# A hybrid attention, state space and expert layer on one core: first products, one gate product, expert choice and one more held weight tile moved

## The reference

```python
h = h + hybrid_mixer(rms_norm(h, norm1_g), ...)   # conv, state space, attention, gates
tok = rms_norm(h, norm2_g)
top_v, top_i = lax.top_k(tok @ w_router + b_router, 4)
top_w = softmax(top_v)
for e in range(32):
    gu = tok @ w_gate_up[e] + b_gate_up[e]         # 1024 x 2048
    gate, up = minimum(gu[:, :1024], 7), clip(gu[:, 1024:], -7, 7)
    act = (up + 1) * (gate * sigmoid(1.702 * gate))
    out += dense_w[:, e:e+1] * (act @ w_down[e] + b_down[e])   # 1024 x 1024
h = rms_norm(h + out, final_g)
```

## Time and profile before

| | us |
|---|---|
| median of 3 timed runs | 1452.72 |
| the runs | 1448.02, 1452.72, 1452.91 |
| the profiled execution | 1448.05 |
| its span, first to last instruction | 1446.2 |
| TensorE busy in the span | 1385.3 |
| VectorE busy | 361.2 |
| ScalarE busy | 233.5 |

### The profile page before, as it was taken

How to read it: one execution, slowest core, us unless ns; L and a number is a source line. 1 busy time by engine, 2 the same in 40 slices (tenths; PEclk the granted TensorE clock), 3 DMA queues, 4 the chain that set the end, 5 groups by cost and what they waited for, 6 DMA issues and landing times.

```text
span 1446.2 us, 14861 instructions
## 1 busy us (share of the span) xinstructions
PE 1385.3 (96%) x6176; PEld 600.4 (42%) x6176; DVE 361.2 (25%) x807; ACT 233.5 (16%) x495; POOL 50.4 (3%) x33
## 2 busy tenths in 40 slices
PE   7999999989999999999999999999999999999997
PEld 6887754444444443333333333333333333333332
DVE  5665855124300122111111111111112112111211
ACT  2116532124300121000100010001001001000101
POOL 1502220000000000000000000000000000000000
PEclk9999999999999999999999999999999999999999
DMA  9455321253156369999999999999999999999995
GB/s 361 178 189 190 117 103 44 115 234 117 68 208 270 146 252 427 426 432 433 433 428 431 433 433 427 430 434 431 430 430 429 431 427 431 429 429 432 432 425 221
DMA packets 25824, 475.01 MB, mean 328 GB/s; under 512 B 4176, under 2 KB 5360, under 8 KB 6800
## 3 DMA queue, kind: packets, MB, share of 16 engines
q1 hardware_dynamic: 25728, 474.28, 78.3%
q10 hardware_dynamic: 48, 0.03, 0.0%
HBM read 473.22 MB, written 1.08 MB: 328 GB/s over the span
## 4 chain that ended last, share of the span: by engine, by line
PE 69%; DMA 29%; DVE 1%; ACT 1%; issue 0%; SPq 0%; DVEq 0%
DMA weights<-in_w_gate_up_dram 28%; PE ps L990 23%; PE ps L673 7%; PE ps L1014 6%; PE ps L553 6%; PE ps L756 4%; PE ps L764 4%; PE ps L578 4%; PE ps L527 2%; PE ps L869 2%; PE ps L847 2%; PE ps L1024 2%; PE ps L950 2%; PE ps L604 1%; PE ps L615 1%; DMA weights<-in_w_blocks_dram 1%
## 5 line engine op out<-in xcount | busy, mean ns | idle before, releaser
L990 PE MATMUL ps<-weights,hnT 128*64 128x512 f32 x2000 | 450.9, 606 | 32.0 <-DMA weights<-in_w_gate_up_dram 32.0
L990 PEld LDWEIGHTS ps<-weights,hnT 128*64 128x64 f32 x2000 | 144.8, 139 | 322.4 <-issue 264.7
L1014 PE MATMUL ps<-weights,hnT 128*64 128x512 f32 x1016 | 225.1, 595 | 1.0 <-ACT hnT L1093 1.0
L1093 ACT ACTIVATE hnT<-ps 128x512 f32<-128x512 f32 (+1 forms) x95 | 49.9, 526 | 785.1 <-PE ps L527 562.0
L1703 DVE TENSOR_SCALAR ssmT<-ps 128x512 f32<-128x512 f32 x32 | 22.1, 692 | 473.6 <-PE ps L990 473.6
L1014 PEld LDWEIGHTS ps<-weights,hnT 128*64 128x64 f32 x1016 | 70.1, 137 | 133.3 <-issue 126.8
L673 PE MATMUL ps<-weights,hnT 128*128 128x512 f32 x224 | 98.0, 594 | 0.0
L553 PE MATMUL ps<-hnT,weights 128*128 128x272 f32 x352 | 81.4, 393 | 0.0
L553 PEld LDWEIGHTS ps<-hnT,weights 128*128 128x128 f32 x352 | 66.7, 190 | 14.0 <-issue 0.4
L1093 ACT ACTIVATE arena<-ps 128x512 f32<-128x512 f32 (+5 forms) x89 | 40.7, 494 | 161.4 <-PE ps L673 81.1
L1024 PE MATMUL ps<-hnT 64*128 64x512 f32 x256 | 63.6, 615 | 0.8 <-DVE hnT L1730 0.8
(11 more groups left out here) (224 smaller groups left out, 920.8 us busy)
## 6 DMA issues: line engine op xcount, KB each, us to landing
weights<-in_w_gate_up_dram SPq DMA_DIRECT2D x53, 4096.0 KB, 20.4
weights<-in_w_down_dram SPq DMA_DIRECT2D x28, 4096.0 KB, 17.4
weights<-in_w_blocks_dram SPq DMA_DIRECT2D x28, 2048.0 KB, 7.9
weights<-in_w_gate_up_dram SPq DMA_DIRECT2D x6, 3072.0 KB, 16.8
weights<-in_w_gate_up_dram SPq DMA_DIRECT2D x8, 2048.0 KB, 8.7
weights<-in_w_down_dram SPq DMA_DIRECT2D x4, 2048.0 KB, 15.4
arena<-in_w_gate_up_dram SPq DMA_DIRECT2D x5, 1024.0 KB, 13.5
weights<-in_w_gate_up_dram SPq DMA_DIRECT2D x4, 1024.0 KB, 7.0
```

The costliest lines, as they stand in the source:

```text
L990: mm = pe.matmul(bank(4 + b)[64 * a:64 * a + 64, :], xe[:, 2 * (k % 4) + k // 4, :], w[:, FF * b + 512 * a:FF * b + 512 * a + 512], start= ...
L1014: mm = pe.matmul(bank(7)[64 * c:64 * c + 64, :], actT[:, P * j + SLOTS * a:P * j + SLOTS * a + SLOTS], pair[kk % 2][:, 512 * c:512 * c + 5 ...
L1093: return nc.scalar.activation(o, i, ACT.Copy)
```

## The change

Five things are changed:

- The first block is laid out in four quarters for tiles 0 to 3, and its first half is requested as two quarters with a semaphore each. TensorE runs 16 products of a matrix of ones ahead of tile 0.
- `filler(1)` stands between `scores(0)` and `scores(1)`, and each pair's filler is the next in number. ScalarE's and VectorE's parts that belong to fillers move one pair forward with them.
- In the expert choice the positions are made ahead of `dense_w`, the constant is added in the table `slots`, and the counts take two products. `start_bias(0)` no longer waits for the tokens. The total count and the turn of `dense_w` stand behind the gather.
- One more chunk is held, for expert 25.
- To make room, some buffers of the expert stage share memory (`act` with `upc`, `actT` with `sig`, `xrow` with `y_sb`), and `bdn` and `gf_bc` are loaded later, to other places.

```diff
-HELD = {18: [("gu", 0)], ..., 24: [("gu", 0)]}
+HELD = {18: [("gu", 0)], ..., 24: [("gu", 0)], 25: [("gu", 0)]}
...
-        "slots": np.tile((SLOTS * np.arange(4)[:, None] + free % SLOTS).reshape(1, -1), (P, 1)),
+        "slots": np.tile((UNROUTED + SLOTS * np.arange(4)[:, None] + free % SLOTS).reshape(1, -1), (P, 1)),
...
-                    sp.dma_start(bdn[0:EXPERTS, :], b_down[0]).then_inc(late_in, 16)
-                    sp.dma_start(gf_bc, final_g.partition_broadcast(P)).then_inc(late_in, 16)
                     load_down(0, 0, upper)
-                    load_held(held_gu[0:3])
+                    load_held(held_gu[0:4])
...
-                    sp.dma_start(weights[:, SLOT:SLOT + SLOT // 2], w_blocks[0, :, 0:SLOT // 2]).then_inc(x0_in, 16)
+                    for j in range(2):
+                        quarter = slice(SLOT // 4 * j, SLOT // 4 * j + SLOT // 4)
+                        sp.dma_start(weights[:, SLOT + quarter.start:SLOT + quarter.stop], w_blocks[0, :, quarter]).then_inc(x0_in[j], 16)
...
+            sp.wait_ge(gate_ps, KD)
+            sp.dma_start(bdn[0:EXPERTS, :], b_down[0]).then_inc(bdn_in, 16)
             sp.wait_ge(os_ps, 8)
+            sp.dma_start(gf_bc, final_g.partition_broadcast(P)).then_inc(gf_in, 16)
             load_held(held_dn)
...
+            pe.wait_ge(zeroed, 3)
+            for i in range(16):
+                pe.matmul(bank(0)[:, 0:P], ones, ones, start=True, stop=True)
             for j in range(CONV_TILES):
-                if j == 0:
-                    pe.wait_ge(x0_in, 16)
+                if j < 2:
+                    pe.wait_ge(x0_in[j], 16)
...
             scores(0)
+            filler(1)
             for p in range(PAIRS):
                 if p + 1 < PAIRS:
                     scores(p + 1)
-                filler(p + 1)
+                filler(p + 2)
...
-            pe.matmul(bank(6)[:, 0:32], tri_lt, routed[:, 0, :], start=True, stop=True)
-            pe.matmul(bank(6)[:, 32:64], ones, routed[:, 0, :], start=True, stop=False)
-            pe.matmul(bank(6)[:, 32:64], tri_lt, routed[:, 1, :], start=False, stop=True).then_inc(route_ps, 1)
+            pe.matmul(bank(7)[:, 0:64], tri_lt, routed.rearrange("p t e -> p (t e)"), start=True, stop=True)
+            pe.matmul(bank(7)[:, 32:64], ones, routed[:, 0, :], start=False, stop=True, skip_group_check=True).then_inc(route_ps, 1)
...
             gather(0)
-            counts()
-            turn_tokens(0)
-            pe.wait_ge(xrow_sb, 1)
-            keep_warm(1)
             pe.wait_ge(bias_part, 6)
+            pe.matmul(bank(4)[:, 0:EXPERTS], ones, routed[:, 0, :], start=True, stop=False)
+            pe.matmul(bank(4)[:, 0:EXPERTS], ones, routed[:, 1, :], start=False, stop=True).then_inc(route_ps, 1)
+            turn_tokens(0, into=6)
             pe.wait_ge(count_ok, 1)
-            start_bias(0)
-            pe.wait_ge(dwT_ok, 1)
+            start_bias(0, first=True)
+            turn_weights()
+            pe.wait_ge(xe_ok, 1)
             unit(0, True, owed=False)
...
-                if 5 <= p < 7:
+                if 4 <= p < 6:
                     dve.wait_ge(gate_ok, 4)
-                    gated_ssm(p - 5, 0)
+                    gated_ssm(p - 4, 0)
```

More of the change, by code:

```diff
@@ L244, in build @@
     selw = split(late[:, 128:384], 2)
-    gmin, sig, upc, act = (late[:, 512 + 512 * i:1024 + 512 * i] for i in range(4))
-    xrow = late[:, 2560:3072]
-    one_hot = split(late[:, 2560:2560 + 96 * OVERFLOW_MAX], OVERFLOW_MAX)
+    gmin, sig, upc = (late[:, 512 + 512 * i:1024 + 512 * i] for i in range(3))
+    act, actT, xrow = upc, sig, y_sb
+    gf_bc = late[:, 2048:3072]
+    one_hot = split(arena[:, 2048:2048 + 96 * OVERFLOW_MAX], OVERFLOW_MAX)
     junk2 = [split(late[:, D * t:D * t + D], 2) for t in range(RT)]
@@ L838, in _ @@
             values(PAIRS - 1)
-            for n in range(PAIRS + 1, 2 * PAIRS):
+            for n in range(PAIRS + 2, 2 * PAIRS):
                 filler(n)
@@ L916, in _, with turn_weights @@
             pe.wait_ge(routed_ok, 1)
[L917 to L924 removed]
+            pe.matmul(bank(7)[:, 0:64], tri_lt, routed.rearrange("p t e -> p (t e)"), start=True, stop=True)
+            pe.matmul(bank(7)[:, 32:64], ones, routed[:, 0, :], start=False, stop=True, skip_group_check=True).then_inc(route_ps, 1)
+            def turn_weights():
                 pe.wait_ge(dense_ok, 1)
+                pe.wait_ge(count_ok, 1)
                 for t in range(RT):
@@ L935, in down_bias @@
             def down_bias(quarters):
+                if quarters:
+                    pe.wait_ge(bdn_in, 16)
                 for n in quarters:
@@ L952, in gather, with turn_tokens, start_bias @@
                 mm.then_inc(xrow_ps2, 1)
-            def turn_tokens(u):
+            def turn_tokens(u, into=5):
                 pe.wait_ge(xrow_sb, u + 1)
                 for j in range(4):
-                    mm = turn(bank(5)[:, P * j:P * j + P], xrow[:, P * j:P * j + P])
+                    mm = turn(bank(into)[:, P * j:P * j + P], xrow[:, P * j:P * j + P])
                 mm.then_inc(xe_ps, 1)
-            def start_bias(u):
-                pe.wait_ge(xe_ok, u + 1)
+            def start_bias(u, first=False):
+                if not first:
+                    pe.wait_ge(xe_ok, u + 1)
                 pe.wait_ge(hot_ok, u + 1)
@@ L994, in turn_selection @@
             def turn_selection(u):
+                if isinstance(u, int) and u == 0:
+                    pe.wait_ge(dwT_ok, 1)
                 pe.wait_ge(selw_ok, u + 1)
@@ L1310, in _ @@
             act_f(hn2[:, 0, :], hrow[:, 0, :], ACT.Copy, scale=rstat[:, 6:7]).then_inc(hn2_ok, 1)
+            act_f(hn2[:, 1, :], hrow[:, 1, :], ACT.Copy, scale=rstat[:, 7:8]).then_inc(hn2_ok, 1)
             act_e.wait_ge(negv_ok, 1)
```

61 lines of the change are left out of this document (28 added, 33 removed).

## The result

The changed kernel takes 1437.86 us (median of 4 runs, 1437.08 to 1438.51); the kernel before took 1452.82 (4 runs, 1448.02 to 1453.04). The ratio is 0.9913, 95% interval 0.9897 to 0.9929. In the three later sets of runs, on other occasions, the kernel before had medians of 1450.26, 1449.81 and 1449.14 (9 runs each), and the changed kernel, once more in the first of them, 1438.66: 0.9919 (0.9905 to 0.9932). The profiled execution took 1438.51 us with a span of 1436.7; it was the slowest of the four, while the profiled one of the kernel before took 1448.05, close to its fastest run (1448.02). The two profiles therefore show less of a difference than the medians do.

What follows compares the result with a forecast made beforehand. TensorE was taken as the bound before about 533 us, then the 431 GB/s weight stream to 1410 us. Terms 3.1 + 4.7 + 1.5 + 2.4 = 11.7 us, off 1450.4, gave 1439 us, range 1434 to 1446.

Steps and rivals of the forecast that it cites:

- First projection: Kernel start: the first weights come as a quarter block, so the first product starts 1.3 us earlier, bounds 0 and 1.4.
- Warming: Ahead of the first tile: 16 products of ones raise TensorE's clock, gaining 1.8 us, bounds 0 and 2.0.
- Rival (a): First tile: the clock isn't held after the warming; gain 9.9 in place of 11.7, 1440.5 us; chance 0.20.
- Attention: Between the first two scores: a gate product fills the 3.0 us wait and removes 1.7 of slow clock; 4.7 us.
- Rival (b): Attention: filling one wait opens another, so the 4.7 us is lost; gain 7.0, 1443.4 us; chance 0.10.
- Expert choice: Before expert 0: gather 0.9 us earlier, expert 0's start 0.6 us closer behind the tokens; 1.5 us, bounds 0.6 and 2.0.
- The eighth tile: Expert stage: expert 25 loads 11 MiB in place of 12, saving 2.4 us of stream, bounds 0 and 2.4.
- All free while the stream is the bound: Expert stage: the held tile's request, later bias and scale loads and shared buffers cost nothing.
- by a hair: Held experts: transfers still set the time, at 26.76 us per expert against TensorE's own period of 26.69.
- if the stream shows gaps or a lower rate: Expert stage: a sign of being wrong; the forecast was a transfer share still 1.00 at 431 GB/s.
- rival (c): Held experts: TensorE sets the time, and eight can each lose a 1.7 us slow stretch; 1452.2 us; chance 0.05.
- all lower bounds without the zeros: Lower gain for the range: 1.3 + 0 + 3.0 + 0.6 + 2.4 = 7.3 us, giving 1445.5 from 1452.8.

Runs made afterwards that it cites:

- spread: The changed kernel with its eight held tiles at experts 16, 18, ... 28 (gate and up) and 30 (down) in place of 18 to 25; 1441.68 us, ratio 0.9940.
- spread_early: The changed kernel with held tiles at experts 16, 18, ... 28 (gate and up) and 25 (down); 1439.40 us, ratio 0.9933.
- down_at_25_again: Second measurement of down_at_25, the changed kernel with the held down tile at expert 25 in place of 22; 1437.60 us, ratio 0.9919.
- Half_block: The changed kernel with the first half block as one request, as before, warming kept; 1439.13 us, ratio 0.9921.
- Old_fillers: The changed kernel with the gate products in their old order, none between the scores of pairs 0 and 1; 1444.10 us, ratio 0.9955.
- down_at_25: The changed kernel with the held down tile at expert 25 in place of 22, gate and up tiles at 18 to 24; 1436.81 us, ratio 0.9918.

## Why the prediction was right, point by point

The forecast was 1439 us in a range of 1434 to 1446; the median is 1437.86. The four parts ahead of the experts came near their forecast, the fifth did not, and that the sum still met the median is in part luck. The parts, from the one profile of each kernel:

- First projection: 1.02 us sooner, 1.3 forecast. Right in kind; the landing varies by as much between executions. The landing was the limit, not the scaled x, which was there at 7.96.
- Warming: 1.93 us, 1.8 forecast, after an idle time of 1.98 us. It held in nine of the eleven profiles that have both warming and quarters; spread and spread_early lost it, after waits of 1.9 us. My reading by the length of the idle time (0.94 us kept the clock, 3.02 lost it) was too simple: down_at_25_again kept it over 2.64 us, spread_early lost it over 1.90. Half_block lost it over 4.1. Rival (a) is thus real in some executions. The medians with and without the warming are 0.4 us apart, so its worth over many executions is not shown.
- Attention: from the meta rows' products to the gate products behind the attention 155.65 against 160.25 us, 4.6, forecast 4.7. Old_fillers confirms it: 6.1 in its profile, 5.2 by the times. Rival (b) fell: no new wait.
- Expert choice: 0.89 us for the gather and 0.61 for the start of expert 0, forecast 0.9 and 0.6. The experiments add that ScalarE's order, which the prediction did not price, is needed for it.
- Together 9.1 us to expert 0, 9.3 forecast.
- The eighth tile: forecast 2.4, measured 1.2 between medians (the intervals of the ratios overlap), 0.9 between like profiles, and 0.2 between the profiles of before and after (878.7 and 878.5 us from expert 0 to expert 31). This is the mis-sized term, and with it the sentence "All free while the stream is the bound". The stream is not the bound throughout. In the held run TensorE and transfers take the same time to 0.07 us, as the prediction noted "by a hair", and a TensorE stretch that is late or slow leaves the engines dry (401 GB/s for 27 us). This is one of the prediction's own signs of being wrong, "if the stream shows gaps or a lower rate". By the time of expert 30's second half the long stretch had used up the whole tile: counted from expert 0, that half starts at 858.4 us in the changed kernel and at 858.0 before. And behind it nothing waits for a transfer in the changed kernel, where before TensorE idled 0.70 us for expert 31's weights (until 1410.42); only that 0.7 was won, so a slow stretch there counts in full. The tail is not the same in each execution: down_at_25 idled 0.26 us ahead of expert 31. This is rival (c)'s mechanism, but it struck once in the held experts, not eight times. That the run's last tail limits the gain is read from the chains; no kernel here removes it.

The sum against the profiled execution came out 9.5 (1448.05 to 1438.51) where 11.7 was forecast. The forecast's start, 1450.4, was 2.4 us above the profiled execution and its sum 2.2 too large, and against the profiled execution of the changed kernel, 1438.51, the two errors cancel: the closeness of 1438.7 is luck. That the median fell by 15.0 in the first set, and by 11.6 in the second, goes with the kernel before's scatter between 1448 and 1453; the changed kernel's nine runs lie within 2.2 us. The 27 later runs of the kernel before show a mean granted clock of 0.988 to 0.990 in the 14 that took under 1449.7 us and of 0.987 to 0.988 in the 13 above, so the slow ones spent more time at the lower clock. In which place, the one profile can't say. Undone one at a time, the parts give 5.2 (attention), 1.2 (tile), 0.4 (warming) and 0.5 us (quarter) between medians, and the expert choice 1.5 between profiles; some 3 of the 11.6 us are in no part that an experiment here isolates.

The range hid the weak term. Its lower end, called "all lower bounds without the zeros", takes the forecast for the first projection (1.3) and for the tile (2.4), though both have 0 as their bound, and takes the 0 for the warming. With the tile at 0 it would have reached to 1452.8 - 4.9 = 1447.9 us.

## What to carry to other kernels

When a stage has one bound on average, look for the places where the second bound is within a per cent: there a saving for the first can be cut short, and a chance delay of the second is kept. Fill a wait with work that is due anyway, and price the slower clock after the wait with the wait; here it was a third of the gain in one profile and half in another. When an operation is moved on one engine, check the order of the engine that feeds it, for half a change can be worse than none.

## What the runs showed of the hardware that was not expected

The same list of instructions meets a different clock from execution to execution. The 32 records of warming took between 5.28 and 6.54 us. After them, an idle time of 2.64 us left the clock up in one execution, and one of 1.90 took it down in another, by the timelines of two kernels that are alike up to there:

```profile
9.08 3.93 PE L558 MATMUL ps<-weights 128*128 128x272 f32 x16 [2.64 <-DMA weights<-in_w_blocks_dram]
```

```profile
9.15 5.62 PE L558 MATMUL ps<-weights 128*128 128x272 f32 x16 [1.90 <-DMA weights<-in_w_blocks_dram]
```

The first is down_at_25_again, the second spread_early. The Trainium skill, "TensorE: Matmul & The Clock Gate", section "Part 1: The HAM clock gate", says that the number of cold products is "run-variable" for the same kernel. The warming agrees: its 32 records took 5.58 us in one execution of the changed kernel and 6.54 in another, against 3.6 for all at the full clock and 7.2 for all at the lower one, both worked out in the prediction. The same holds later in the program: ahead of expert 30's second half an idle time of 2.24 us left the clock up in the changed kernel (7.09 us for the 32 records), and one of 2.12 took it down in down_at_25_again (8.78). So a length of idle time alone doesn't tell whether the clock is kept, and a single profile of such an edit can be off by the whole 1.7 to 1.9 us either way.
